# First phase of a two-block transformer kernel: both modulation vectors as column products on TensorE

## The chip, the cores and the metric

The kernel runs on one core of a Trainium2 chip, with float32 data. The metric is the device time of one execution in microseconds. A core has TensorE (PE, with its weight loads shown apart as PEld), VectorE (DVE), ScalarE (ACT), GpSimd (POOL) and SyncE (SP), each with its own instruction stream, tied together by semaphores; 16 DMA engines move data between HBM and the on-chip memory. TensorE writes to PSUM only.

## What is computed

Two blocks of layers on a sequence of 256 tokens of width 1024. What matters here is how the first one begins:

```python
def modulate(h, shift, scale):
    return h * (1.0 + scale[:, None, :]) + shift[:, None, :]

c_act = jax.nn.silu(c)
for i in range(DEPTH):
    mod = c_act @ ada_w[i] + ada_b[i]
    sh1, sc1, g1, sh2, sc2, g2, sh3, sc3, g3 = jnp.split(mod, N_MOD, axis=-1)
    h = modulate(rms_norm(x, ln_ffn1[i]), sh1, sc1)
    x = x + 0.5 * g1[:, None, :] * swiglu(h, ffn1_wg[i], ffn1_wu[i], ffn1_wd[i])
    ...
```

`sh1` is vector 0 of the kernel, `sc1` vector 1, `g1` vector 2. Each is a product of a row of 1024 with a 1024 x 1024 block of `ada_w`, 4 MB in float32. The first matrix product of the layer, `h @ wg`, needs vectors 0 and 1; `g1` is needed at the end of the layer.

## The kernel before

**Phases.** The program goes through ten phases, F0 (the first SwiGLU layer) first. Activations are kept with the feature on the partition: 8 blocks (`KB`) of 128 features by 256 tokens. Weights come in slabs of 128 x 2048, 1 MB each, into six slots (`raw`). ScalarE rounds a slab (`split_hi`), VectorE takes the remainder (`split_lo`), and TensorE makes three products for each pair of blocks: high by high, low by high, high by low.

**Vectors.** A block of `ada_w` comes as 8 tiles of 128 x 1024, 512 KB, each with two DMAs of 256 KB (`ada_load`, L2049). An interleaving is used: a tile holds `AG` = 2 halves j, each 128 partitions by 512 columns, where the parity of a partition tells which half of the output columns it holds. `ada_tile` (L2784, L2787) lets VectorE multiply a half by one column of c and add it to an accumulator, 16 steps for a vector. `ada_sum` (L2398) then sums over the partitions on TensorE: four calls with 128 columns of the accumulator stationary and the two columns of `group_ones` moving. The tiles are numbered m: vector 1 has 0 to 7, vector 0 has 8 to 15, vector 2 begins at 16. Tiles 4 to 11 lie in the slots of slabs 2 to 5, all others in the four slots of `ada` (m mod 4).

**The start, vector 1.** VectorE sums all 8 tiles into an accumulator of its own. `ada_sum(1)` puts it into PSUM (`first_summed`), and `mod_vector(1)` adds the bias (L2796).

**The start, vector 0.** VectorE sums tiles 8 to 11. For 12 to 15 (`PE_TILES` = 4) TensorE makes the product itself, `shift_tile` (L2499): two columns of `c_pair` stationary, 512 columns of the tile moving, into a 2 x 512 row in PSUM. `shift_start` (L2507) adds VectorE's part to the same row. ScalarE copies the row (L2626), `shift_turn` (L2514) transposes it in four pieces, and `mod_vector(0)` adds the bias. `c_pair` holds, for each of the 16 halves, a column of c masked by parity.

**TensorE's order at the start.** 16 transposes of x (L2524), 16 warm-up calls (`keep_warm`, L2406: ones by the identity into a bank that nobody reads), the sums of squares for rms_norm (L2425, 16 calls), 16 warm-up calls, six transposes of parameter rows (L2534), the spreading of 1/rms over the partitions (L2439), `ada_sum(1)`, 16 warm-up calls, the shift tiles and the turn, and then slab 0: `first_product` (L2297, L2303), which waits for the rounded operand (`norm_hi`). Slab 1 follows with `col_product` (L2270 to L2272).

**Queues.** SyncE issues c, x, the 16 tiles, and slabs 0 and 1; slab 0 goes ahead of tile 15. A load into a slot that is used again waits for `ada_step`, VectorE's count of steps. Slabs 2 to 5 wait for the tiles in their place. GpSimd issues the parameter rows, then vector 2's first four tiles (each waits for `ada_taken`, the count of tiles that TensorE has taken), then fills the table of distances for the attention phase (L2198, 32 copies, two DMAs), then vector 2's other tiles. VectorE sums vector 2 between the splits of F0.

Of the kernel before, what the change touches and what calls it, by code (L numbers as in the profile page):

```python
# [35 lines left out]
P = 128  # L36
# [3 lines left out]
KB = D // P  # L40
# [6 lines left out]
WARM = 8  # L47
ATILES = 4
AG = 2
AW = D // AG  # L50
AQ = P // AG
ASTEPS = KB * AG
PE_TILES = KB // 2
N_MOD = 9
# [53 lines left out]
def build(nc, T, out):  # L108
    phases = PHASES
    nslabs = sum(SLABS_OF.get(p, FFN_SLABS) for p in phases)  # L110
    with ExitStack() as ctx:
# [38 lines left out]
        def view(a, b):  # L150
            return work[:, a:b]
# [41 lines left out]
        def bank(t, j):  # L193
            return t[:, j * 512:(j + 1) * 512]
# [133 lines left out]
        out_rows = view(0, 2048)  # L328
        shift_row = view(5120, 5632)
        silu_sb = view(4096, 4608)  # L330
# [1671 lines left out]

        def acc_of(v):

            return view(8192, 8192 + AW) if v == 1 else ada_acc[:, 0:AW]

        first_summed, first_turned = bank(up, 1)[:, 0:KB], bank(up, 0)[:, 0:KB]

        def tile_index(v, k):

            return (v if v >= 2 else 1 - v) * KB + k

        def tile_steps(m):

            return AG * (m if m < 2 * KB else m - PE_TILES)

# [21 lines left out]
        def ada_load(eng, v, k, it=0, source=None):  # L2038
            m = tile_index(v, k)
            full = tile_full(m)[0]  # L2040
            if m >= 2 * KB + ATILES:
                eng.wait_ge(S["ada_step"], tile_steps(m - ATILES + 1) + ASTEPS * it)
            elif m >= 2 * KB:
                eng.wait_ge(S["ada_taken"], m - ATILES + 1 - (2 * KB - PE_TILES))
            elif m >= ATILES + 8:
                eng.wait_ge(S["ada_step"], tile_steps(m % ATILES + 1))
            source = ada_source(v, k) if source is None else source
            for j in range(AG):
                eng.dma_start(ada_place(m)[:, j * AW:(j + 1) * AW],  # L2049
                              source[j * AQ:(j + 1) * AQ, :].rearrange("q (g n) -> q g n", g=AG)).then_inc(full, 16)  # L2050

        @block.sync
        def _(sp):
            early_slabs = []
            def load(s, it, sources):

                if s >= RAW:
                    sp.wait_ge(lo_done, s - RAW + 1 + RAW * it)
                elif s >= 2:
                    sp.wait_ge(S["ada_step"], tile_steps(2 * s + 2))  # L2060
                for place, src in sources:
                    sp.dma_start(place(slab(raw, s, RAW)), src).then_inc(raw_full[s % RAW], 16)
# [47 lines left out]
            for k in range(KB):  # L2110
                if k == KB - 1:
                    load(0, 0, up_src(phases[0], 0, 0))
                ada_load(sp, 0, k)
# [58 lines left out]
        def _(pool):  # L2172
# [17 lines left out]
            link(pool.memset(rel_rows[0:HEADS, :], -1e30))  # L2190
            for k in range(ATILES):
                ada_load(pool, FIRST_VEC[phases[0]], k)
            pool.wait_ge(S["rel_rows"], 16)
# [24 lines left out]
            for p in phases:  # L2218
# [7 lines left out]
                if p in FFNS:  # L2226
                    if p in FIRST_VEC:
                        v = FIRST_VEC[p]
                        for k in range(ATILES, KB):
                            ada_load(pool, v, k)  # L2230
# [32 lines left out]
        def _(pe):  # L2263
# [127 lines left out]
            def ada_sum(v, it=0, o=bank(misc, 1)):  # L2391
# [5 lines left out]
                for h in range(KB // AG):  # L2397
                    last = pe.matmul(by_group[:, :, h], acc_of(v)[:, h * P:(h + 1) * P], group_ones[:, :],  # L2398
                                     start=True, stop=True, skip_group_check=True)
# [91 lines left out]

            def shift_tile(k):

                m = tile_index(0, k)
                full, count = tile_full(m)
                pe.wait_ge(full, count)
                for j in range(AG):
                    i = k * AG + j
                    last = pe.matmul(bank(misc, 1)[0:AG, :], c_pair[:, i * AG:(i + 1) * AG], ada_place(m)[:, j * AW:(j + 1) * AW],  # L2499
                                     start=(k == KB - PE_TILES and j == 0), stop=(k == KB - 1 and j == AG - 1),  # L2500
                                     skip_group_check=True)
                last.then_inc(S["ada_taken"], 1)

            def shift_start():

                pe.wait_ge(S["ada_step"], tile_steps(2 * KB - PE_TILES))
                pe.matmul(bank(misc, 1)[0:AG, :], group_ones[:, :], acc_of(0), start=False, stop=False, skip_group_check=True)  # L2507

            def shift_turn():

                pe.wait_ge(S["start_act"], 3)
                by_group = first_turned[:, 0:KB].rearrange("p (g h) -> p g h", g=AG)
                for h in range(KB // AG):
                    last = pe.transpose(by_group[:, :, h], shift_row[0:AG, h * P:(h + 1) * P], ident[0:AG, 0:AG])  # L2514
                last.then_inc(S["ada_summed"], 1)

# [5 lines left out]
            for k in range(KB):  # L2522
# [3 lines left out]
                if k % 2:  # L2526
                    last.then_inc(S["x_turned"], 1)
            keep_warm(bank(up, 0), 2 * WARM)
            norm_sums(phases[0], wide=False)
            keep_warm(bank(up, 0), 2 * WARM)  # L2530
            pe.wait_ge(S["rows_loaded"], 16 * len(rows_plan))
# [9 lines left out]
            pe.wait_ge(S["c_spread"], 2)  # L2541
            for k in range(KB - PE_TILES, KB):
                if k == KB - 1:
                    shift_start()
                shift_tile(k)
            shift_turn()
            for p in phases:
# [19 lines left out]
        def _(act):  # L2567
# [18 lines left out]
            def norm(name):  # L2586
# [30 lines left out]
                if n == 0:  # L2617
# [124 lines left out]
        def _(dve):  # L2742
# [28 lines left out]
            def ada_tile(v, k, it=0):  # L2771
# [4 lines left out]
                if k == 0 and v > 1:  # L2776
                    dve.wait_ge(S["ada_summed"], v + it)
                acc = acc_of(v)
                for j in range(AG):
# [18 lines left out]
            def norm(name):  # L2798
# [29 lines left out]
                if n == 0:  # L2828
                    split_lo(0)
                    mod_vector(0, psum=first_turned)  # L2830
                if name == "G":
# [90 lines left out]
            def ffn(p):  # L2922
# [92 lines left out]
                if v is not None and not more:  # L3015
# [10 lines left out]
                              group_ones[:, :].unsqueeze(1).to_broadcast([P, ASTEPS, AG]), ALU.mult).then_inc(S["c_spread"], 1)  # L3026
            for k in range(KB):
                ada_tile(1, k)
                if k == KB - 2:
                    dve.wait_ge(S["sqrt_done"], 1)  # L3030
                    dve.reciprocal(rstd, rstd).then_inc(S["rstd_done"], 1)
            for k in range(KB - PE_TILES):
                ada_tile(0, k)
            dve.wait_ge(S["start_act"], 2)
            for i, o in enumerate(OUT_COL.values()):
# [4 lines left out]
                                   float(NSA_HD) ** -0.5, ALU.mult, ALU.mult))  # L3040
            mod_vector(1, psum=first_summed)
            for p in phases:
# [26 lines left out]
```

## Time and profile before

| | us |
|---|---|
| median of 3 runs | 1780.62 |
| lowest, highest | 1780.35, 1782.24 |
| the profiled execution, its time | 1784.23 |
| the profiled execution, its span | 1782.6 |

Busy in the span: TensorE 1728.5 us, VectorE 1434.3, ScalarE 912.5, GpSimd 407.6. The DMA engines moved 411.44 MB, 231 GB/s in the mean. Times in the rows are counted from the span's start. A row of the timeline may merge several instructions (x32); its length is that of all of them. A float32 matmul of the program leaves two records of the weight load and two of the matmul. The granted clock is the share of 2.4 GHz that the throttle left to TensorE; 0.50 is 1.2 GHz.

### The profile page before, as it was taken

The page shows a single profiled execution, that of the slowest core. Times are in us where ns is not written, and L with a number is a line of the kernel's source. Part 1 is how long each engine was busy: PE and PEld are TensorE (multiplying, and loading weights), DVE is VectorE, ACT ScalarE, POOL GpSimd, SP SyncE. Part 2 cuts the span into 40 slices and gives each one's busy share as a digit, 9 for nine tenths or more (in the row PEclk, how much of TensorE's full clock was granted, in tenths as well). Part 3 has the DMA queues.
Part 4 walks back from the last instruction along what each step waited for, and adds up shares of the span by engine and source line. Part 5 has one row for each costly group of instructions (what it writes and reads, how often), then busy time and mean ns, then how long its engine had stood idle before and what let it go on. Part 6 is the DMA issues. An engine that isn't in the chain of part 4 may idle for free. (4 is left out here: it accounts for less than half of the span.)

```text
span 1782.6 us, 36482 instructions
## 1 busy us (share of the span) xinstructions
PE 1728.5 (97%) x14077; PEld 1682.8 (94%) x14077; DVE 1434.3 (80%) x1850; ACT 912.5 (51%) x1274; POOL 407.6 (23%) x669
## 2 busy tenths in 40 slices
PE   7999999999999999999999999899999998899998
PEld 6999999999999999989999998899999997699998
DVE  6777898688779888868977899869988998678555
ACT  3433377764335433456533366566444656665444
POOL 5322311013223222120122344411322121301000
PEclk9999999999999999999999999999999998999999
DMA  9998857448986888756698856335989592147550
GB/s 336 358 340 272 301 186 259 154 169 311 322 282 237 287 292 299 253 192 210 239 327 273 298 186 224 106 119 190 322 299 294 142 240 95 48 131 257 168 188 24
DMA packets 261792, 411.44 MB, mean 231 GB/s; under 512 B 21950, under 2 KB 204414, under 8 KB 261560
## 3 DMA queue, kind: packets, MB, share of 16 engines
q1 hardware_dynamic: 224968, 290.67, 49.1%
q0 software_dynamic: 36720, 119.36, 19.0%
q8 instruction: 69, 1.13, 0.3%
q14 instruction: 35, 0.29, 0.1%
HBM read 408.90 MB, written 2.63 MB: 231 GB/s over the span
## 5 line engine op out<-in xcount | busy, mean ns | idle before, releaser
L2751 DVE TENSOR_TENSOR lo<-raw,hi 128x2048 fp32r<-128x2048 f32 (+1 forms) x257 | 581.6, 2265 | 186.1 <-ACT hi L2578 185.8
L2578 ACT CAST hi<-raw 128x2048 fp32r<-128x2048 f32 (+1 forms) x266 | 498.7, 1878 | 393.2 <-PE dacc L2272 194.7
L2270 PE MATMUL up<-operand_hi,hi 128*128 128x256 f32 x1952 | 554.0, 284 | 4.0 <-DVE lo L2751 3.9
L2271 PE MATMUL up<-operand_lo,hi 128*128 128x256 f32 x1952 | 553.2, 283 | 0.0
L2272 PE MATMUL up<-operand_hi,lo 128*128 128x256 f32 x1952 | 553.0, 283 | 0.0
L2049 POOL DMA_DIRECT2D ada<-in_ada_w_dram x448 | 259.9, 597 | 816.9 <-DVE ada_acc L2787 753.4
L2270 PEld LDWEIGHTS up<-operand_hi,hi 128*128 128x128 f32 x1952 | 375.3, 192 | 5.5 <-DVE lo L2751 5.0
L2272 PEld LDWEIGHTS up<-operand_hi,lo 128*128 128x128 f32 x1952 | 375.4, 192 | 0.0
L2271 PEld LDWEIGHTS up<-operand_lo,hi 128*128 128x128 f32 x1952 | 375.3, 192 | 0.0
L2787 DVE SCALAR_TENSOR_TENSOR ada_acc<-ada,c_col,ada_acc 128x512 f32<-128x512 f32 x420 | 318.8, 759 | 13.5 <-DVE ada_acc L2787 0.5
L2270 PE MATMUL dacc<-act_hi,hi 128*128 128x256 f32 x1056 | 298.9, 283 | 2.6 <-DVE act_lo L2964 2.6
L2272 PE MATMUL dacc<-act_hi,lo 128*128 128x256 f32 x1056 | 298.5, 283 | 0.0
L2271 PE MATMUL dacc<-act_lo,hi 128*128 128x256 f32 x1056 | 297.8, 282 | 0.0
L2270 PEld LDWEIGHTS dacc<-act_hi,hi 128*128 128x128 f32 x1056 | 200.0, 189 | 3.2 <-issue 2.2
L2271 PEld LDWEIGHTS dacc<-act_lo,hi 128*128 128x128 f32 x1056 | 198.8, 188 | 0.0
L2272 PEld LDWEIGHTS dacc<-act_hi,lo 128*128 128x128 f32 x1056 | 198.0, 187 | 0.0
L2213 POOL TENSOR_TENSOR work<-work 128x256 f32<-128x256 f32 x52 | 40.1, 771 | 344.7 <-ACT work L2604 342.4
L2270 PE MATMUL dacc<-operand_hi,hi 128*128 128x256 f32 x352 | 101.3, 288 | 3.4 <-DVE operand_lo L843 2.4
L2272 PE MATMUL dacc<-operand_hi,lo 128*128 128x256 f32 x352 | 99.6, 283 | 0.0
L2271 PE MATMUL dacc<-operand_lo,hi 128*128 128x256 f32 x352 | 99.6, 283 | 0.0
L2680 ACT ACTIVATE work<-up 128x512 f32<-128x512 f32 x41 | 24.5, 598 | 136.0 <-PE up L2272 136.0
L2270 PEld LDWEIGHTS dacc<-operand_hi,hi 128*128 128x128 f32 x352 | 67.4, 192 | 4.7 <-issue 3.7
(455 smaller groups left out, 2716.0 us busy)
## 6 DMA issues: line engine op xcount, KB each, us to landing
ada<-in_ada_w_dram POOLq DMA_DIRECT2D x448, 256.0 KB, 4.6
raw<-in_ffn_wg_dram SPq DMA_DIRECT2D x88, 512.0 KB, 5.4
raw<-in_ffn_wu_dram SPq DMA_DIRECT2D x88, 512.0 KB, 5.0
raw<-in_ffn_wd_dram SPq DMA_DIRECT2D x88, 512.0 KB, 5.4
raw<-in_ffn_w_up_dram SPq DMA_DIRECT2D x88, 512.0 KB, 4.5
raw<-in_ffn_w_down_dram SPq DMA_DIRECT2D x46, 512.0 KB, 4.4
raw<-in_hg_w_in_dram SPq DMA_DIRECT2D x32, 512.0 KB, 5.9
raw<-in_attn_w_qkv_dram SPq DMA_DIRECT2D x24, 512.0 KB, 7.5
```

The lines of the kernel that those rows point to most:

```text
L2049: eng.dma_start(ada_place(m)[:, j * AW:(j + 1) * AW], source[j * AQ:(j + 1) * AQ, :].rearrange("q (g n) -> q g n", g=AG)).then_inc(full, 16)
L2213: ins = pool.tensor_tensor(acc, op_k(squares, 0) if k == 1 else acc, op_k(squares, k), ALU.add)
L2270: pe.matmul(o, stat[0], mov[0], start=start, stop=False, skip_group_check=True)
L2271: pe.matmul(o, stat[0], mov[1], start=False, stop=False, skip_group_check=True)
L2272: return pe.matmul(o, stat[1], mov[0], start=False, stop=stop, skip_group_check=True)
L2578: last = act.copy(put(slab(hi, s, SPL)), take(slab(raw, s, RAW)))
L2680: act.activation(silu_sb, bank(up, 0), ACT.Silu).then_inc(S["silu_done"], 1)
L2751: last = dve.tensor_tensor(put(slab(lo, s, SPL)), take(slab(raw, s, RAW)), put(slab(hi, s, SPL)).bitcast(F32), ALU.subtract)
L2787: dve.scalar_tensor_tensor(acc, t, c, acc, ALU.mult, ALU.add).then_inc(S["ada_step"], 1)
```

## The change

Vectors 1 and 0 both go through TensorE from the first tile to the last. `first_tile` takes a tile as it lies: 128 x 128 blocks of it are stationary, and the two columns of `c_pair` for this half move. A half has four such blocks, a tile eight, and all 64 calls of a vector add up in one 128 x 8 region of PSUM, which `mod_vector` reads. Behind each tile stand two warm-up calls. `first_done` is one more warm-up call whose end tells VectorE that the region is complete. VectorE's steps for vectors 1 and 0, the copy by ScalarE and the turn are gone. The loads that waited for `ada_step` wait for `ada_taken`. Slab 0 is issued ahead of tile 14 instead of tile 15. GpSimd loads vector 2 behind the table of distances and behind the first use of a slab (`slab_used`).

```diff
-PE_TILES = KB // 2
+PE_TILES = 2 * KB
...
-        first_summed, first_turned = bank(up, 1)[:, 0:KB], bank(up, 0)[:, 0:KB]
+        first_summed = {1: bank(up, 1)[:, 0:KB], 0: bank(misc, 1)[:, 0:KB]}
...
             elif m >= ATILES + 8:
-                eng.wait_ge(S["ada_step"], tile_steps(m % ATILES + 1))
+                eng.wait_ge(S["ada_taken"], m % ATILES + 1)
...
                 elif s >= 2:
-                    sp.wait_ge(S["ada_step"], tile_steps(2 * s + 2))
+                    sp.wait_ge(S["ada_taken"], 2 * s + 2)
...
-                if k == KB - 1:
+                if k == KB - 2:
                     load(0, 0, up_src(phases[0], 0, 0))
...
-            for k in range(ATILES):
-                ada_load(pool, FIRST_VEC[phases[0]], k)
             pool.wait_ge(S["rel_rows"], 16)
...
-                        for k in range(ATILES, KB):
+                        if p == phases[0]:
+                            pool.wait_ge(slab_used, 1)
+                        for k in range(0 if p == phases[0] else ATILES, KB):
                             ada_load(pool, v, k)
...
+            def first_tile(v, k):
+
+                m = tile_index(v, k)
+                full, count = tile_full(m)
                 pe.wait_ge(full, count)
+                by_group = first_summed[v].rearrange("p (g h) -> p g h", g=AG)
                 for j in range(AG):
                     i = k * AG + j
...
+                    for h in range(KB // AG):
+                        last = pe.matmul(by_group[:, :, h], ada_place(m)[:, j * AW + h * P:j * AW + (h + 1) * P],
+                                         c_pair[:, i * AG:(i + 1) * AG], start=(k == 0 and j == 0 and h == 0),
+                                         stop=(k == KB - 1 and j == AG - 1), skip_group_check=True)
                 last.then_inc(S["ada_taken"], 1)
...
+            def first_done():
+
+                pe.matmul(bank(up, 0)[:, 0:P], ones[:, :], ident[:, :], start=True, stop=True,
+                          skip_group_check=True).then_inc(S["ada_summed"], 1)
...
-            keep_warm(bank(up, 0), 2 * WARM)
+            pe.wait_ge(S["c_spread"], 2)
+            for k in range(5):
+                first_tile(1, k)
+                keep_warm(bank(up, 0), 2)
             norm_sums(phases[0], wide=False)
-            keep_warm(bank(up, 0), 2 * WARM)
+            for k in range(5, KB):
+                first_tile(1, k)
+                keep_warm(bank(up, 0), 2)
+            first_done()
...
-            ada_sum(1, o=first_summed)
-            keep_warm(bank(up, 0), 2 * WARM)
...
-            shift_turn()
+            for k in range(KB):
+                first_tile(0, k)
+                if k < KB - 1:
+                    keep_warm(bank(up, 0), 2)
+            first_done()
+            keep_warm(bank(up, 0), WARM // 2)
...
-                    act.wait_ge(S["ada_taken"], PE_TILES)
-                    act.copy(shift_row[0:AG, :], bank(misc, 1)[0:AG, :]).then_inc(S["start_act"], 1)
...
-            for k in range(KB):
-                ada_tile(1, k)
-                if k == KB - 2:
-                    dve.wait_ge(S["sqrt_done"], 1)
-                    dve.reciprocal(rstd, rstd).then_inc(S["rstd_done"], 1)
-            for k in range(KB - PE_TILES):
-                ada_tile(0, k)
+            dve.wait_ge(S["sqrt_done"], 1)
+            dve.reciprocal(rstd, rstd).then_inc(S["rstd_done"], 1)
```

TensorE, from the transposes of x to the first transpose of the parameter rows, before (x16 is that many calls; `ident,ones` is a warm-up call, `ones,work` a sum of squares):

```order
L2524 MATMUL dacc<-ident,work 128x128 x16
L2406 MATMUL up<-ident,ones 128x128 x16
L2425 MATMUL misc<-ones,work 128x128 x16
L2406 MATMUL up<-ident,ones 128x128 x16
L2534 MATMUL dacc<-ident,work 128x128
```

and of the changed kernel, from the same place to the sums of squares:

```order
L2513 MATMUL dacc<-ident,work 128x128 x16
L2496 MATMUL up<-c_pair,ada 128x2 x8
L2401 MATMUL up<-ident,ones 128x128 x2
L2496 MATMUL up<-c_pair,ada 128x2 x8
L2401 MATMUL up<-ident,ones 128x128 x2
L2496 MATMUL up<-c_pair,ada 128x2 x8
L2401 MATMUL up<-ident,ones 128x128 x2
L2496 MATMUL up<-c_pair,ada 128x2 x8
L2401 MATMUL up<-ident,ones 128x128 x2
L2496 MATMUL up<-c_pair,raw 128x2 x8
L2401 MATMUL up<-ident,ones 128x128 x2
L2420 MATMUL misc<-ones,work 128x128 x16
```

Five tiles now stand where one block of warm-up calls was; the other three of vector 1 follow the sums of squares.

TensorE, the end of the phase up to the first product of slab 0, before:

```order
L2398 MATMUL up<-group_ones,work 128x2 x4
L2406 MATMUL up<-ident,ones 128x128 x16
L2499 MATMUL misc<-ada,c_pair 2x512 x6
L2507 MATMUL misc<-ada_acc,group_ones 2x512
L2499 MATMUL misc<-ada,c_pair 2x512 x2
L2514 MATMUL up<-ident,work 128x2 x4
L2297 MATMUL up<-operand_hi,hi 128x256
```

and of the changed kernel, its last three tiles:

```order
L2496 MATMUL misc<-c_pair,ada 128x2 x8
L2401 MATMUL up<-ident,ones 128x128 x2
L2496 MATMUL misc<-c_pair,ada 128x2 x8
L2401 MATMUL up<-ident,ones 128x128 x2
L2496 MATMUL misc<-c_pair,ada 128x2 x8
L2503 MATMUL up<-ident,ones 128x128
L2401 MATMUL up<-ident,ones 128x128 x4
L2292 MATMUL up<-operand_hi,hi 128x256
```

The joining product and the four transposes are gone, and the closing call stands directly behind the last tile.

## Rows read from the trace of the kernel before

**Rows 1.** The page: busy us of an engine, share of the span, instructions.

```profile
PE 1728.5 (97%) x14077; PEld 1682.8 (94%) x14077; DVE 1434.3 (80%) x1850; ACT 912.5 (51%) x1274; POOL 407.6 (23%) x669
```

**Rows 2.** Waits of TensorE, 0 to 100 us: total, times, longest.

```profile
PE up L2270 <- DVE lo L2751: 2.0, 1, 2.0
```

**Rows 3.** Windows: PE, PEld, DVE, ACT, POOL busy; granted clock; DMA share; GB/s.

```profile
10.00:20.00 10.00, 10.00 (x92) 10.00 (x91) 9.04 (x13) 5.00 (x13) 4.92 (x10) 1.00 1.07 371
...
34.00:36.00 2.00, 1.16 (x4) 0.24 (x4) 0.39 (x1) 1.57 (x1) 0.83 (x2) 1.00 1.08 372
...
46.00:48.00 2.00, 1.11 (x7) 1.12 (x8) 0.83 (x1) 1.59 (x1) 1.70 (x6) 0.86 1.09 361
...
48.00:50.00 2.00, 2.00 (x11) 2.00 (x11) 1.66 (x1) 1.97 (x3) 1.88 (x3) 0.50 1.03 398
...
50.00:52.00 2.00, 2.00 (x16) 2.00 (x15) 0.63 (x1) 2.00 (x2) 1.53 (x5) 0.78 1.06 362
```

**Rows 4.** Timeline of the start: start us, us, engine, line, what [idle before].

```profile
9.74 0.49 DVE L2784 TENSOR_SCALAR work<-ada,c_col 128x512 f32<-128x512 f32 x1 [5.60 <-DMA ada<-in_ada_w_dram]
...
9.94 3.65 PEld L2406 LDWEIGHTS up<-ident,ones 128*128 128x128 f32 x32
...
20.77 0.98 PE L2534 MATMUL dacc<-ident,work 128*128 128x128 f32 x6
...
21.58 0.64 PE L2439 MATMUL misc<-ident,small 128*128 128x128 f32 x4
...
22.69 0.97 PEld L2398 LDWEIGHTS up<-group_ones,work 128*128 128x128 f32 x8 [0.66 <-DVE work L2787]
...
35.07 1.88 PE L2499 MATMUL misc<-ada,c_pair 128*2 128x512 f32 x4 [0.84 <-DMA ada<-in_ada_w_dram]
...
38.06 0.17 DVE L2796 TENSOR_TENSOR modcol<-up,cols 128x8 f32<-128x8 f32 x1 [0.16 <-PE up L2514]
...
38.91 0.35 PE L2297 MATMUL up<-operand_hi,hi 128*128 128x256 f32 x1 [0.89 <-ACT operand_hi L2634]
```

**Rows 5.** Timeline, product of slab 1.

```profile
46.88 0.39 PE L2270 MATMUL up<-operand_hi,hi 128*128 128x256 f32 x1 [1.99 <-DVE lo L2751]
...
48.11 0.41 PE L2271 MATMUL up<-operand_lo,hi 128*128 128x256 f32 x1
...
48.32 0.41 PE L2272 MATMUL up<-operand_hi,lo 128*128 128x256 f32 x1
...
51.84 0.28 PE L2271 MATMUL up<-operand_lo,hi 128*128 128x256 f32 x1
...
51.96 0.28 PE L2272 MATMUL up<-operand_hi,lo 128*128 128x256 f32 x1
```

**Rows 6.** Timeline of phase N: float32 rows with few moving columns.

```profile
1438.98 2.08 PE L1625 MATMUL dacc<-work 128*64 128x60 f32 x32
...
1453.04 3.65 PE L1638 MATMUL misc<-work 128*128 128x30 f32 x32
...
1456.63 3.26 PE L1625 MATMUL dacc<-work 128*64 128x60 f32 x32
```

**Rows 7.** Windows behind the second of those rows, columns as in 3.

```profile
1457.00:1458.00 1.00, 1.00 (x15) 1.00 (x13) 0.99 (x2) 0.52 (x1) 0.00 (x0) 0.58 0.12 45
...
1460.60:1461.00 0.40, 0.40 (x6) 0.40 (x5) 0.37 (x2) 0.00 (x0) 0.00 (x0) 1.00 0.89 174
```

**Rows 8.** Weight loads by form, 1505.0 to 1507.4 us, then 1495.0 to 1496.5.

```profile
L1694 PEld LDWEIGHTS dacc<-work 128*64 128x64 f32 x5 | 1.1, 231 | 0.5 <-issue 0.5
...
L1694 PEld LDWEIGHTS dacc<-work 128*64 128x64 f32 x8 | 1.0, 136 | 0.6 <-issue 0.3
```

**Rows 9.** Vector 2: a load, its first use; page, us to landing.

```profile
30.54 1.22 POOL L2049 DMA_DIRECT2D ada<-in_ada_w_dram  x2 [15.61 <-PE misc L2499]
...
64.83 0.48 DVE L2784 TENSOR_SCALAR ada_acc<-ada,c_col 128x512 f32<-128x512 f32 x1
...
ada<-in_ada_w_dram POOLq DMA_DIRECT2D x448, 256.0 KB, 4.6
```

More of the change, by code:

```diff
@@ L328, in build @@
         out_rows = view(0, 2048)
-        shift_row = view(5120, 5632)
         silu_sb = view(4096, 4608)
@@ L1999, in build @@
         PE_MIX["N"], ACT_MIX["N"], DVE_MIX["N"] = pe_nsa, act_nsa, dve_nsa
-        def acc_of(v):
-            return view(8192, 8192 + AW) if v == 1 else ada_acc[:, 0:AW]
-        first_summed, first_turned = bank(up, 1)[:, 0:KB], bank(up, 0)[:, 0:KB]
+        first_summed = {1: bank(up, 1)[:, 0:KB], 0: bank(misc, 1)[:, 0:KB]}
         def tile_index(v, k):
@@ L2013, in tile_steps @@
         def tile_steps(m):
-            return AG * (m if m < 2 * KB else m - PE_TILES)
+            return AG * (m - PE_TILES)
         def tile_full(m):
@@ L2043, in ada_load @@
             elif m >= 2 * KB:
-                eng.wait_ge(S["ada_taken"], m - ATILES + 1 - (2 * KB - PE_TILES))
+                eng.wait_ge(S["ada_taken"], m - ATILES + 1)
             elif m >= ATILES + 8:
-                eng.wait_ge(S["ada_step"], tile_steps(m % ATILES + 1))
+                eng.wait_ge(S["ada_taken"], m % ATILES + 1)
             source = ada_source(v, k) if source is None else source
@@ L2397, in ada_sum @@
                 for h in range(KB // AG):
-                    last = pe.matmul(by_group[:, :, h], acc_of(v)[:, h * P:(h + 1) * P], group_ones[:, :],
+                    last = pe.matmul(by_group[:, :, h], ada_acc[:, h * P:(h + 1) * P], group_ones[:, :],
                                      start=True, stop=True, skip_group_check=True)
@@ L2489, in ffn @@
                     ada_sum(v + 4)
-            def shift_tile(k):
-                m = tile_index(0, k)
+            def first_tile(v, k):
+                m = tile_index(v, k)
                 full, count = tile_full(m)
                 pe.wait_ge(full, count)
+                by_group = first_summed[v].rearrange("p (g h) -> p g h", g=AG)
                 for j in range(AG):
                     i = k * AG + j
-                    last = pe.matmul(bank(misc, 1)[0:AG, :], c_pair[:, i * AG:(i + 1) * AG], ada_place(m)[:, j * AW:(j + 1) * AW],
-                                     start=(k == KB - PE_TILES and j == 0), stop=(k == KB - 1 and j == AG - 1),
-                                     skip_group_check=True)
+                    for h in range(KB // AG):
+                        last = pe.matmul(by_group[:, :, h], ada_place(m)[:, j * AW + h * P:j * AW + (h + 1) * P],
+                                         c_pair[:, i * AG:(i + 1) * AG], start=(k == 0 and j == 0 and h == 0),
+                                         stop=(k == KB - 1 and j == AG - 1), skip_group_check=True)
                 last.then_inc(S["ada_taken"], 1)
[L2504 to L2515, printed above, removed]
+            def first_done():
+                pe.matmul(bank(up, 0)[:, 0:P], ones[:, :], ident[:, :], start=True, stop=True,
+                          skip_group_check=True).then_inc(S["ada_summed"], 1)
             pe.wait_ge(S["c_spread"], 1)
@@ L2538, in _ @@
             spread(misc[:, SEQ:2 * SEQ], rstd).then_inc(S["spread"], 1)
-            ada_sum(1, o=first_summed)
-            keep_warm(bank(up, 0), 2 * WARM)
[L2541 to L2545, printed above, removed]
-            shift_turn()
+            for k in range(KB):
[4 more added lines that the diff above has]
+            keep_warm(bank(up, 0), WARM // 2)
             for p in phases:
@@ L2777, in ada_tile @@
                     dve.wait_ge(S["ada_summed"], v + it)
-                acc = acc_of(v)
+                acc = ada_acc[:, 0:AW]
                 for j in range(AG):
@@ L2829, in norm @@
                     split_lo(0)
-                    mod_vector(0, psum=first_turned)
+                    mod_vector(0, psum=first_summed[0])
                 if name == "G":
@@ L3040, in _ @@
                                    float(NSA_HD) ** -0.5, ALU.mult, ALU.mult))
-            mod_vector(1, psum=first_summed)
+            mod_vector(1, psum=first_summed[1])
             for p in phases:
```

## The prediction

> **What bounds the kernel now.** I read the page first, then the waits of TensorE, then the first 50 us row by row. TensorE is busy for 97% of the span [rows 1], so what delays it is paid in full and what another engine saves is worth nothing unless TensorE waited for it. In the first 100 us it has few waits; the one that counts is 2.0 us for the remainder of slab 1 [rows 2]. Before the first product the start is paced by transfers. The DMA engines are full at 371 GB/s [rows 3], a tile of a modulation vector is 2 x 256 KB, so one lands every 0.524 MB / 371 GB/s = 1.41 us, and the last one lands just ahead of 35.07, where TensorE takes it up. VectorE keeps that pace, and the engine that has room is TensorE: most of its rows up to 28 us are warm-up products on constants (48 calls). After the last tile come 1.88 us of products, the copy of the row by ScalarE, four small transposes, the addition of the bias at 38.06 and the first product of slab 0 at 38.91 [rows 4]. I call that last moment T0. Everything the change does lies ahead of T0, apart from the wait for slab 1 and the clock just behind it. From there the program is the same, so the result is the move of T0, corrected for those two.
>
> **The unit of the sum.** A float32 matmul on a 128-column stationary leaves two records in the trace: 16 warm-up calls are 32 records. At the full clock (2.4 GHz) they follow each other every (3.65 - 0.19)/31 = 0.112 us. The new kind of product is already in the trace too, in the sum of vector 1: four calls with 128 stationary columns and two moving ones, 8 records, (0.97 - 0.19)/7 = 0.111 us apart [rows 4]. So a product that moves two columns costs as much as one that moves 128; its weight load sets the time. I use 0.112 for both. The old shift products (2 stationary columns, 512 moving) cost 1.88 us for 4 records, one tile: 16 records of the new kind in a tile cost 1.79 us, about the same.
>
> **What is removed.** From TensorE: 48 warm-up calls, the sum of vector 1 (8 records), four tiles of the old form with their join, and four small transposes, all ahead of T0. Of these only what follows the last landing was on the path. From VectorE: 12 tile sums of vectors 1 and 0. They ran beside the transfers at the pace of the landings and did not set T0, so nothing is gained there. The way from the last old product (35.07 + 1.88 = 36.95) to the bias at 38.06 loses its copy and its turn, 1.1 us, if the last tile were still what ends the phase. It isn't, as the next sum shows.
>
> **What is added.** Per tile 8 calls, 16 records; 16 tiles are 256 records. Two warm-up calls behind each tile but the last: 15 x 4 = 60. The sums of squares stay, 32, and two closing calls add 4. That is 352 records. The six transposes of parameter rows and the two that spread rstd keep about 1.3 us [rows 4]. A tile with its warm-up calls takes 20 x 0.112 = 2.24 us where one lands every 1.41. TensorE becomes the bound of the whole phase, and the tiles of both vectors stand in one line on it.
>
> **T0 at the full clock.** TensorE is free of the x transposes at about 10.05 and tile 0 has landed by 9.74 [rows 4]. 10.05 + 352 x 0.112 (39.4) + 1.3 = 50.8. From the bias to the first product it took 0.85 us before; with the hop from the closing call I take 0.9. T0 = 51.7, which is 12.8 later than 38.91. The four warm-up calls ahead of slab 0 (0.9) fit into that hop.
>
> **The clock.** The new rows load weights nearly all the time and move few columns. Very similar rows exist in the later part of this kernel: 32 records with 128 stationary and 30 moving columns from 1453.04, back to back, then 32 with 64 and 60 [rows 6]. TensorE never idled there, and yet the granted clock went from 1.00 to 0.50 (1.2 GHz) about 4.1 us after they began, and back at about 1460.6, once dense products ran again [rows 7]. Twenty of those records move 600 columns; twenty of the new ones, warm-up calls included, move 16 x 2 + 4 x 128 = 544. So I expect the low level here as well. How long a record takes there: dense products with 128 columns loaded stood 0.21 us apart at 0.50 (48.11 to 48.32) against 0.12 at 1.00 (51.84 to 51.96, [rows 5]), and a load of 64 columns took 231 ns instead of 136 at a place where the moving side was the longer one [rows 8], so the loads themselves slow down. No row shows a two-column product at the low clock. From below it costs 0.112 as at full clock, from above 0.213, double the nearest row; I take 0.213, since the load is what sets it and the load was seen to slow by about that step.
>
> The page "TensorE: Matmul & The Clock Gate" of the Trainium skill, section "LDWEIGHTS (loading the stationary operand)", gives a load as columns / 1.2 ns with no mention of the clock's state, thus 107 ns; the trace agrees at full clock (0.111) and speaks against it at the low one (231 ns against 136). That rule is the second rival below.
>
> **T0 with the clock as those rows had it.** I let it fall 4 us after a run of tiles begins and return 4 us after dense rows begin. First five tiles from 10.05: 36 records until 14.1, then 64 x 0.213 = 13.6, to 27.7. Sums of squares: 19 records low, 13 at full, 5.5, to 33.2. Three tiles: 36 records, then 24 low, to 42.3. Closing call, transposes and spread, all taken double: 3.0, to 45.3. Eight tiles: 156 x 0.213 = 33.2, to 78.5. Closing call 0.4 and hop 0.9: T0 = 79.8, which is 40.9 later. Dense rows began at 78.5, so slab 0 runs at the low clock until 82.5, 2.7 us, and loses 2.7 x (1 - 0.12/0.213) = 1.2.
>
> **Behind T0.** Before, TensorE waited 1.99 us ahead of 46.88 for slab 1 [rows 5], and its clock was at 0.50 for 3.4 us soon after (0.86, 0.50 and 0.78 in [rows 3]), which cost 3.4 x (1 - 0.12/0.213) = 1.5. In the new kernel slabs 0 and 1 have landed long ahead. With slab 0 slowed no wait is left, so 2.0 + 1.5 = 3.5 is given back; at the full clock ScalarE still rounds slab 1 after the eight operand rows, and I leave 1.0 of the 2.0 (bounds 0 and 2). Net: 40.9 + 1.2 - 3.5 = **+38.6 us**.
>
> **Moved at no cost.** GpSimd no longer waits for tiles before its table of distances, and loads vector 2 once slab 0 has been used, about 6 us after T0. A tile is two issues, 1.22 us together (four tiles: 4.9), and lands 4.6 us after its issue in the median [rows 9], so four tiles are there by T0 + 16. VectorE first uses one at 64.83, T0 + 26 [rows 9]: ten microseconds of cover; without it VectorE would hold back the next split by what is missing. Queued behind GpSimd's wait are only these loads. SyncE's loads of slabs 2 to 5 now wait for tiles taken by TensorE instead of VectorE; tile 12 is taken before T0 by several tiles, so they land under the phase.
>
> **The rivals.** *Full clock throughout:* the warm-up calls hold it. For it speaks that between 34 and 36 us TensorE was busy for 1.16 of 2 us and the clock stayed at 1.00 [rows 3], and that the new phase has no gap. Against it, rows 6 and 7. It gives 12.8 - 1.0 - 1.5 = +10.3. The same page, in "Why this matters for your kernels", ties drops to idle gaps between bursts; by that rule this rival would be the outcome, but the clock fell at 1457 with TensorE busy throughout. *The clock falls, the loads don't slow:* only records that move 128 columns double. That adds to 51.7: 49 warm-up records in the low stretches (244 x 4/20) x 0.1 = 4.9, sums of squares 1.9, transposes and closing calls 1.7; T0 = 60.2, net 21.3 + 1.2 - 3.5 = +19.0. This also stands for a clock that is low for part of the time only. *Faster:* the load of the next two-column product hides, and TensorE keeps pace with the landings. It decides at (1.41 - 0.45)/16 = 0.060 us for a record; that is the step of records with 64 stationary columns ((2.08 - 0.22)/31, [rows 6]), not of 128. T0 would be 10.05 + 256 x 0.060 + 96 x 0.112 + 1.3 + 0.9 = 38.4, -0.5, and net -0.5 - 1.0 - 1.5 = -3.0; with faster records still the last landing limits it to about -4.
>
> **How the numbers follow.** The profiled execution has a span of 1782.6 and a time of 1784.23, 3.6 over the median of the runs, 1780.62. The shifts are in microseconds of the same work, so I add them to the median. Low clock: 66%, 1780.6 + 38.6 = 1819.2. Partly low, or loads not slowed: 12%, 1799.6. Full clock: 18%, 1790.9. TensorE keeps pace: 4%, 1777. About 0.2% (3.6 us) is what a measurement of this kernel can tell from no change; the last case lies on that border and is split: faster 0.02, same 0.02, slower 0.96. If all of the phase ran at the low clock: 352 x 0.213 + 2.6 + 10.05 + 0.9 = 88.6, net +47.4, 1828. The range takes in this and the full-clock rival with 2 us below it: 1789 to 1828.
>
> **What would show it.** The granted clock in the windows from 14 to 78 us: 0.50 in most for the forecast, 1.00 for the first rival. The new product line: 0.213 us a record at the low clock, 0.112 at full; a record of 0.112 at 0.50 is the second rival. The first product of slab 0 at about 80 (forecast), 60, 52 or 38. No wait for slab 1, no wait of VectorE for vector 2. The forecast fails if the clock holds, or if the records are shorter than the four in the sum of vector 1.

## The result, and the profile after

| | before | changed |
|---|---|---|
| median, us | 1780.63 (4 runs) | 1822.56 (4 runs) |
| lowest, highest | 1780.35, 1782.24 | 1821.91, 1824.48 |
| span of the profiled execution | 1782.6 | 1820.3 |

The ratio is 1.023, 95% interval 1.0216 to 1.0243: 41.9 us slower between the medians, 37.7 between the two profiled spans. The forecast was 1819.2 (+38.6).

TensorE in the first 100 us of the changed kernel has no wait behind the arrival of x; the wait for slab 1 of [rows 2] is gone. The granted clock tells the rest (windows of the changed kernel; columns as in [rows 3]):

```profile
12.00:16.00 4.00, 4.00 (x27) 4.00 (x28) 0.00 (x0) 3.39 (x10) 3.63 (x12) 0.71 1.06 367
16.00:20.00 4.00, 4.00 (x21) 4.00 (x21) 0.00 (x0) 0.00 (x0) 2.96 (x18) 0.50 1.06 367
...
28.00:32.00 4.00, 4.00 (x20) 4.00 (x20) 0.00 (x0) 0.00 (x0) 0.57 (x1) 0.50 1.08 365
32.00:36.00 4.00, 4.00 (x29) 4.00 (x29) 0.17 (x1) 0.26 (x1) 0.00 (x0) 0.73 1.05 426
36.00:40.00 4.00, 4.00 (x38) 4.00 (x37) 0.00 (x0) 0.00 (x0) 0.00 (x0) 1.00 0.98 307
40.00:44.00 4.00, 4.00 (x24) 3.60 (x23) 0.00 (x0) 0.00 (x0) 0.00 (x0) 0.62 0.98 315
44.00:48.00 4.00, 4.00 (x21) 4.00 (x20) 2.28 (x10) 3.07 (x8) 0.00 (x0) 0.50 0.63 219
...
72.00:76.00 4.00, 4.00 (x20) 4.00 (x21) 0.00 (x0) 0.00 (x0) 0.00 (x0) 0.50 0.00 0
...
80.00:84.00 4.00, 4.00 (x29) 4.00 (x28) 3.23 (x8) 4.00 (x8) 0.00 (x0) 0.76 0.00 0
```

TensorE is busy for 4.00 of 4.00 us in every one of these windows and yet has 20 or 21 products in a window at 0.50 where it has 38 in the one at 1.00. The clock is at 0.50 from 13.7 to 34.2 and from 41.0 to 82.0 us.

The timeline of TensorE, the rows that answer to [rows 4] (L2496 is the column product, L2401 a warm-up call):

```profile
7.44 3.32 PE L2513 MATMUL dacc<-ident,work 128*128 128x128 f32 x16 [3.63 <-DMA work<-in_x_dram]
10.60 1.84 PE L2496 MATMUL up<-c_pair,ada 128*128 128x2 f32 x16
...
29.12 6.14 PE L2420 MATMUL misc<-ones,work 128*128 128x128 f32 x32
35.10 1.84 PE L2496 MATMUL up<-c_pair,raw 128*128 128x2 f32 x16
37.33 1.84 PE L2496 MATMUL up<-c_pair,raw 128*128 128x2 f32 x16
...
45.26 3.41 PE L2496 MATMUL misc<-c_pair,raw 128*128 128x2 f32 x16
...
49.52 3.41 PE L2496 MATMUL misc<-c_pair,raw 128*128 128x2 f32 x16
52.80 1.20 PE L2401 MATMUL up<-ident,ones 128*128 128x128 f32 x4
53.79 3.41 PE L2496 MATMUL misc<-c_pair,raw 128*128 128x2 f32 x16
...
75.12 3.41 PE L2496 MATMUL misc<-c_pair,ada 128*128 128x2 f32 x16
78.40 0.77 PE L2503 MATMUL up<-ident,ones 128*128 128x128 f32 x2
78.97 1.91 PE L2401 MATMUL up<-ident,ones 128*128 128x128 f32 x8
80.53 0.56 PE L2292 MATMUL up<-operand_hi,hi 128*128 128x256 f32 x1
```

A tile with its two warm-up calls takes 37.33 - 35.10 = 2.23 us at the full clock and 53.79 - 49.52 = 4.27 at the low one: 20 records of 0.112 and of 0.213. The sixteen tiles follow each other without a gap on TensorE, with the sums of squares and the transposes of the parameter rows between them, and slab 0 begins at 80.53 instead of 38.91. Behind it, the same instruction of VectorE, the remainder of the first hidden activations, first in the kernel before, then in the changed one:

```profile
55.81 0.69 DVE L2964 TENSOR_TENSOR act_lo<-work,act_hi 128x512 fp32r<-128x512 f32 x1 [0.69 <-ACT act_hi L2695]
```

```profile
94.32 0.69 DVE L2955 TENSOR_TENSOR act_lo<-work,act_hi 128x512 fp32r<-128x512 f32 x1 [0.69 <-ACT act_hi L2686]
```

94.32 - 55.81 = 38.51 us: of the 41.6 by which slab 0 starts later, 3.1 are given back within the first two slabs, and from here to 750 us the two traces run side by side at that distance, within 0.04. Behind that it shrinks to 37.7 in three small steps, near 757, 801 and 1623 us of the trace of before. The windows around them have the clock at 1.00 in both traces, so the clock is not their reason, and what it is stays open.

### The profile page after: what moved, and what is told of

Read it like the earlier page. It is cut to its first block and busy times, and to the rows that moved or that the text cites. A ratio compares the mean times of both kernels' runs of the same rounds, so it can differ in the third digit from the quotient of the medians.

```text
span 1820.3 us, 36852 instructions
## 1 busy us (share of the span) xinstructions
PE 1771.7 (97%) x14279; PEld 1733.1 (95%) x14279; DVE 1416.9 (78%) x1826; ACT 911.5 (50%) x1273; POOL 400.9 (22%) x669
## 5 line engine op out<-in xcount | busy, mean ns | idle before, releaser
L2778 DVE SCALAR_TENSOR_TENSOR ada_acc<-ada,c_col,ada_acc 128x512 f32<-128x512 f32 x420 | 318.9, 759 | 13.7 <-DVE ada_acc L2778 0.6
```

The source lines that it names most:

```text
L2778: dve.scalar_tensor_tensor(acc, t, c, acc, ALU.mult, ALU.add).then_inc(S["ada_step"], 1)
```

## The experiments

Three kernels ask for the clock, the other runs for the rest of the change and for what stays open. "Before" is run with each batch; its medians were 1782.1, 1782.6 and 1780.7 us in the three, with single executions from 1778.0 to 1786.6, so comparisons go by the ratio within a batch.

**Move 128 columns instead of two.** The columns of c are repeated 64 times. The load and the 16 records of a tile's products stay, the warm-up calls behind the tiles go. The result is wider, so the addition of the bias picks its two columns out of each 128.

```diff
-                        last = pe.matmul(by_group[:, :, h], ada_place(m)[:, j * AW + h * P:j * AW + (h + 1) * P],
-                                         c_pair[:, i * AG:(i + 1) * AG], start=(k == 0 and j == 0 and h == 0),
+                        last = pe.matmul(first_summed[v][:, h * P:(h + 1) * P].rearrange("p (r g) -> p r g", g=AG),
+                                         ada_place(m)[:, j * AW + h * P:j * AW + (h + 1) * P],
+                                         c_pair[:, i * AG:(i + 1) * AG].unsqueeze(1).to_broadcast([P, WIDE, AG]), start=(k == 0 and j == 0 and h == 0),
```

> The changed kernel with 128 columns moving instead of 2: the two columns of c_pair are repeated 64 times, into four 128-column regions of the bank, of which two columns each are read. The warm-up calls behind the tiles are taken out. The output is the reference's. Clock theory (a record costs 0.112 us at the full clock whether it moves 2 or 128 columns, and the rows with few moving columns let the clock fall): the granted clock stays at 1.00, 292 records x 0.112 = 32.7 from 10.6, + 1.3 + 0.9, slab 0's first product at about 45.5, time 1785 (1783 to 1788). Rival (the phase is long for another reason: waits for tiles, the weight load itself slower from tiles than from the accumulator): first product at 65 to 80, time 1805 to 1822.

Measured: 1788.23 us (6 runs), ratio to before 1.0031 (1.0014 to 1.0048), about +5.5 us. The windows and the timeline:

```profile
20.00:24.00 4.00, 4.00 (x39) 4.00 (x38) 0.00 (x0) 0.25 (x1) 2.42 (x11) 1.00 1.05 383
...
36.00:40.00 4.00, 4.00 (x38) 4.00 (x37) 1.56 (x1) 0.00 (x0) 0.00 (x0) 1.00 0.97 294
```

```profile
30.42 7.31 PE L2496 MATMUL misc<-c_pair,raw 128*128 128x128 f32 x64
37.57 7.31 PE L2496 MATMUL misc<-c_pair,ada 128*128 128x128 f32 x64
...
45.99 0.35 PE L2293 MATMUL up<-operand_hi,hi 128*128 128x256 f32 x1
```

Four tiles are 64 records in 7.15 us, 0.112 each, with 64 times as many columns moved. Slab 0 begins at 45.99 against 45.5 expected, and from 12 us on the clock is at 1.00 by the windows and by the records both; the first two microseconds of tiles ran slower, with 11 products from 10 to 12 us. The clock theory holds: of the 42 us, some 36 go with the clock and the 60 warm-up records (6.7 at full clock) that this kernel leaves out; what is left is TensorE's 1.79 us for a tile that lands every 1.41. The next kernel leaves out the same records and moves two columns. The two differ only in the columns moved and in how the bias picks up the result, so the step between them, 1788.23 against 1811.28, is that of the columns.

**Leave the warm-up calls out.**

```diff
             for k in range(5):
                 first_tile(1, k)
-                keep_warm(bank(up, 0), 2)
             norm_sums(phases[0], wide=False)
             for k in range(5, KB):
                 first_tile(1, k)
-                keep_warm(bank(up, 0), 2)
             first_done()
...
                 first_tile(0, k)
-                if k < KB - 1:
-                    keep_warm(bank(up, 0), 2)
             first_done()
```

> The changed kernel without the two warm-up calls behind each tile, nothing else. Clock theory: they did not hold the clock, so the 60 records go at 0.213 us each: first product 12.8 earlier than 80.5, at 67.7, time 1822.6 - 12.8 = 1810. Rival (they keep part of the phase at the full clock): the time stays within 3 us of 1822.6 or rises.

Measured: 1811.28 us (1805.8 to 1818.5, 4 runs), ratio 1.0159 (1.0129 to 1.019), so 11 us under the changed kernel by the medians and 13 by the ratios, with 12.8 expected. By the times the warm-up calls cost their records and held nothing. The trace is less clear. In it slab 0 began at 73.31, not 67.7, and TensorE had the full clock for 3.4 us of the phase, where it had it for 10 in the changed kernel. Whether the missing calls or this one execution made that difference is not shown.

The clock did not come up at the x transposes at all, and the first 23 us of tiles ran at the low level. This is read from the records, not from the clock column:

```profile
10.26 13.65 PE L2496 MATMUL up<-c_pair,ada 128*128 128x2 f32 x64
```

```profile
12.00:16.00 4.00, 4.00 (x20) 4.00 (x20) 0.00 (x0) 3.10 (x10) 3.63 (x12) 1.00 1.06 365
...
34.00:38.00 4.00, 4.00 (x32) 4.00 (x31) 0.17 (x1) 0.12 (x1) 0.00 (x0) 0.81 0.96 364
44.00:48.00 4.00, 4.00 (x22) 4.00 (x20) 3.52 (x13) 2.40 (x5) 0.00 (x0) 0.50 0.63 211
```

From 12 to 16 us the column says 1.00, but there are 20 products, as many as at 0.50 elsewhere, and the first 64 records take 13.65 us, 0.213 each. In this trace the column stands at 1.00 from the start until the first fall that it shows, at 36.5 us, though the records go from 0.213 to 0.112 at 33.1. So ahead of the first change in a trace the column alone proves nothing, and the distance of the records has to be looked at with it.

**Eight warm-up calls instead of two.** 180 more records.

```diff
-                keep_warm(bank(up, 0), 2)
+                keep_warm(bank(up, 0), 8)
```

(in all three places)

> The changed kernel with eight warm-up calls instead of two behind each tile: 180 more records. Clock theory: the denser mix keeps the clock at 1.00, 532 records x 0.112 = 59.6 from 10.6, + 1.3 + 0.9, first product at 72.4, time 1822.6 - 8 = 1814, faster although work is added. Rival (cost goes by the number of records, the clock is not what matters or still falls): 180 x 0.213 = 38 later, time 1861.

Measured: 1813.3 us (1811.7, 1811.8, 1814.8 and 1830.2), ratio 1.0205 (1.0165 to 1.0244). Slab 0 begins at 72.09, expected 72.4, and all windows of the phase are at 1.00:

```profile
28.00:32.00 4.00, 4.00 (x39) 4.00 (x38) 0.00 (x0) 0.03 (x1) 0.50 (x1) 1.00 1.08 364
...
60.00:64.00 4.00, 4.00 (x37) 4.00 (x37) 0.00 (x0) 0.00 (x0) 0.00 (x0) 1.00 1.09 357
```

```profile
65.45 1.84 PE L2496 MATMUL misc<-c_pair,ada 128*128 128x2 f32 x16
67.16 2.03 PE L2401 MATMUL up<-ident,ones 128*128 128x128 f32 x16
...
72.09 0.35 PE L2292 MATMUL up<-operand_hi,hi 128*128 128x256 f32 x1
```

Each tile has 32 records instead of 20 and takes 3.58 us instead of 4.27. In the phase more work takes less time, 8.4 us less, and the rival's 38 us more are far off. This tells the clock from the count of records more sharply than anything else here. For the whole kernel the gain is not shown: three of the four executions lie 8 to 11 us under the median of the changed kernel, but one lies above it, and the interval of the ratio takes in the changed kernel's 1.023.

**The part on GpSimd's queue alone.** The kernel before, with vector 2's loads behind the table of distances and behind slab 0:

```diff
-            for k in range(ATILES):
-                ada_load(pool, FIRST_VEC[phases[0]], k)
             pool.wait_ge(S["rel_rows"], 16)
...
-                        for k in range(ATILES, KB):
+                        if p == phases[0]:
+                            pool.wait_ge(slab_used, 1)
+                        for k in range(0 if p == phases[0] else ATILES, KB):
                             ada_load(pool, v, k)
```

> The kernel before with one part of the change alone: GpSimd loads vector 2 behind the table of distances and behind the first use of a slab. Transfer theory (the 2.1 MB of vector 2 lay ahead of slab 1 and delayed it by up to 2.1 MB / 371 GB/s = 5.6 us): the wait of 2.0 us for slab 1 goes, the clock no longer falls behind it (1.5 us), time 1777 (1776 to 1779). Rival (slab 1 came late for another reason, or the clock falls anyway): no change, 1780.6 within 0.7.

> The same kernel as e1_pool, on the chip of this batch, to compare e5 and e6 with. The wait of 2.0 us for slab 1 is gone and the clock falls once, ahead of or under slab 0: -1 to -2 us against the kernel before, ratio 0.9990 to 0.9995. If it comes out at 1.0000 or above, the wait that went is paid back elsewhere.

Measured: 1780.8 us and 0.9992 (0.9981 to 1.0004) the first time, 1780.41 and 0.9988 (0.9979 to 0.9996) the second, 12 runs each: -1.4 and -2.1 us. The first interval takes in no change, the second just does not; the 1777 us expected were not reached. The wait for slab 1 fell from 2.0 to nothing and to 0.8. Windows of the first, where TensorE's longest wait behind 10 us is 0.9, for ScalarE's first operand row:

```profile
38.00:40.00 2.00, 1.26 (x10) 1.29 (x11) 1.43 (x5) 1.91 (x5) 0.00 (x0) 1.00 1.10 348
40.00:42.00 2.00, 2.00 (x12) 2.00 (x11) 1.91 (x5) 2.00 (x5) 0.00 (x0) 0.50 1.13 413
42.00:44.00 2.00, 2.00 (x13) 2.00 (x13) 0.79 (x1) 2.00 (x2) 0.00 (x0) 0.65 0.99 407
```

The wait is gone and the clock fell all the same, now under slab 0. In the second execution of the same program it did not fall there. The 1.5 us that I had charged to the wait for slab 1 thus do not hang on that wait alone. The two executions also show where single executions of this kernel come to differ by some microseconds. Their spans are 1782.1 and 1776.3, and the windows of the later phases differ in the clock, first of the one, then of the other:

```profile
336.00:340.00 4.00, 3.79 (x20) 3.82 (x21) 2.07 (x6) 3.15 (x9) 0.00 (x0) 0.62 0.37 130
1183.00:1187.00 4.00, 4.00 (x23) 4.00 (x23) 1.56 (x3) 0.00 (x0) 0.00 (x0) 0.57 0.70 241
```

```profile
336.00:340.00 4.00, 4.00 (x35) 4.00 (x36) 2.32 (x5) 3.13 (x9) 0.00 (x0) 1.00 0.27 92
1183.00:1187.00 4.00, 4.00 (x37) 4.00 (x35) 0.64 (x1) 1.36 (x2) 0.00 (x0) 1.00 0.00 0
```

**Fill the gaps ahead of slab 0.** e1_pool with warm-up calls where TensorE waits for ScalarE:

```diff
+            keep_warm(bank(up, 0), 3)
             shift_turn()
+            keep_warm(bank(dacc, 0), 4)
```

> e1_pool with three warm-up calls while ScalarE copies the shift row and four behind the turn, where TensorE sits idle anyway; nothing else. If the gaps between the shift products and slab 0 are what lets the clock fall under slab 0 (39.98 to 43.40 us in e1_pool), it stays at 1.00 and the time is 1.5 us under e1_pool, ratio to before 0.998. If the shift products themselves (two stationary columns, 28 to 37 us) are what lowers it, the clock falls as in e1_pool and the time is that of e1_pool.

Measured: 1782.51 us, ratio 0.9992 (0.9982 to 1.0002). The clock stayed at 1.00 from 38 to 44 us, but it did so in the second execution of e1_pool too, without the calls. Slab 0 began at 39.28 against 38.74. Inconclusive on the clock, and no gain.

**Column products only for the last four tiles.** The kernel before with the moved loads, and tiles 12 to 15 as column products with 128 columns moving. VectorE's sum of tiles 8 to 11 joins as four more products; copy and turn are gone, and three warm-up calls stand ahead of slab 0.

```diff
                 for j in range(AG):
                     i = k * AG + j
-                    last = pe.matmul(bank(misc, 1)[0:AG, :], c_pair[:, i * AG:(i + 1) * AG], ada_place(m)[:, j * AW:(j + 1) * AW],
+                    for h in range(KB // AG):
+                        last = pe.matmul(wide_out(h), ada_place(m)[:, j * AW + h * P:j * AW + (h + 1) * P],
+                                         wide_in(c_pair[:, i * AG:(i + 1) * AG]),
...
-                    act.wait_ge(S["ada_taken"], PE_TILES)
-                    act.copy(shift_row[0:AG, :], bank(misc, 1)[0:AG, :]).then_inc(S["start_act"], 1)
```

> The kernel before with vector 2's loads moved as in e1_pool, and the last four tiles of vector 0 as column products with 128 columns moving; VectorE's share of vector 0 joins them as four more products, the bias is added straight from PSUM as soon as the last tile is taken. Theory (where the last landing ends the phase, the copy and the turn are worth 1.1 us, and columns moving without a pause hold the clock): first product at 37.9 against 38.9, no wait for slab 1 (2.0), clock at 1.00 behind it (1.5), together -4.5 us against the kernel before of the same batch, ratio 0.9975. Rival (the column tiles at 1.79 us do not keep up with the last landings, or the clock falls at the wait for the last tile all the same): first product at 38.5 to 39.5, -1 to -2.5 us, ratio 0.9985 to 0.9995.

Measured: 1780.69 us, ratio 0.9988 (0.9978 to 0.9998), no better than the moved loads alone, where I had expected 0.9975. The timeline tells why the copy and the turn were worth nothing:

```profile
33.79 1.90 ACT L2589 CAST hi<-raw 128x2048 fp32r<-128x2048 f32 x1 [4.41 <-DMA raw<-in_ffn_wg_dram]
35.20 2.05 PE L2509 MATMUL misc<-c_pair,ada 128*128 128x128 f32 x16 [0.58 <-DMA ada<-in_ada_w_dram]
35.72 2.29 DVE L2760 TENSOR_TENSOR lo<-raw,hi 128x2048 fp32r<-128x2048 f32 x1 [2.71 <-ACT hi L2589]
37.09 0.39 PE L2524 MATMUL up<-ident,ones 128*128 128x128 f32 x2
37.93 0.16 DVE L2802 TENSOR_TENSOR modcol<-misc,cols 128x8 f32<-128x8 f32 x1
38.78 0.36 PE L2306 MATMUL up<-operand_hi,hi 128*128 128x256 f32 x1 [0.63 <-ACT operand_hi L2643]
```

The last tile is done at 37.1, but the bias (L2802) comes at 37.93, where VectorE has come through the split of slab 0 (L2760), 2.29 us from 35.72; in VectorE's program the split stands ahead of the bias. So it stood before:

```profile
35.61 2.29 DVE L2751 TENSOR_TENSOR lo<-raw,hi 128x2048 fp32r<-128x2048 f32 x1 [2.73 <-ACT hi L2578]
```

There the split ran to 37.9, and the bias came at 38.06, 0.16 us later, behind the turn [rows 4]. All but these 0.16 us of the copy and the turn were hidden beside it.

**The same with two columns moving.**

```diff
-        WIDE = 64
+        WIDE = 1
```

> e5_hybrid with 2 columns moving instead of 128 in the last four tiles, nothing else; the number of records is the same. Clock theory: from about 28 to 37 us few columns move, the clock falls in or just behind that stretch and rows run at 0.213 instead of 0.112 for some 3.4 us or more, so the time is 1.5 to 6 us over e5_hybrid. Rival (a run of four tiles is too short to matter): equal to e5_hybrid within 0.7 us.

Measured: 1783.96 us (10 runs), ratio 1.0008 (0.9997 to 1.0019), 3.3 over e5_hybrid. In the trace the clock fell at 30.6, two microseconds into the four tiles, and stayed down until 47.7; slab 0 began at 44.00. This is the slowest of the ten executions (1789.86 us; the others 1782.0 to 1785.6), so it shows the effect larger than it is in the median.

```profile
28.00:32.00 4.00, 3.33 (x24) 3.36 (x25) 3.83 (x13) 0.31 (x1) 2.64 (x7) 0.82 1.09 361
32.00:36.00 4.00, 4.00 (x20) 4.00 (x20) 1.47 (x4) 1.72 (x1) 0.00 (x0) 0.50 1.08 362
```

```profile
28.67 8.64 PE L2509 MATMUL misc<-c_pair,ada 128*128 128x2 f32 x48 [1.28 <-DMA ada<-in_ada_w_dram]
44.00 0.56 PE L2306 MATMUL up<-operand_hi,hi 128*128 128x256 f32 x1
```

Forty-eight records take 8.64 us, in e5_hybrid 5.60, where the clock stays at 1.00 through the phase. The two kernels differ in nothing but the number of columns moved, and four tiles are enough to set it off.

**Slab 0 one tile earlier**, on top of e5_hybrid, the line of the change on SyncE's queue:

```diff
-                if k == KB - 1:
+                if k == KB - 2:
                     load(0, 0, up_src(phases[0], 0, 0))
```

> e5_hybrid with slab 0 issued ahead of tile 14 instead of tile 15 (the one line of the change on that queue). In e5_hybrid the last tile was taken at 37.09 but the bias came at 37.93, directly behind VectorE's split of slab 0. Theory (that split bounds the phase there): it ends some 1.4 us earlier, the bias comes at 37.2, the first product at 38.1 instead of 38.78, time 0.7 us under e5_hybrid. Rival (the last tile lands later by what slab 0 gains): the first product stays at 38.6 to 39.2 and the time is that of e5_hybrid.

Measured: 1784.17 us, ratio 1.0012 (1.0002 to 1.0021), about 4 us slower than e5_hybrid by the ratios. The rival was right, and by more than it said:

```profile
34.37 2.05 PE L2509 MATMUL misc<-c_pair,ada 128*128 128x128 f32 x16 [1.82 <-DMA ada<-in_ada_w_dram]
37.15 1.95 PE L2509 MATMUL misc<-c_pair,ada 128*128 128x128 f32 x16
39.14 0.17 DVE L2802 TENSOR_TENSOR modcol<-misc,cols 128x8 f32<-128x8 f32 x1 [1.92 <-PE misc L2509]
```

The split now ends at 37.2, but tile 14 is taken at 34.37, behind a wait of 1.8 us, and tile 15 at 37.15 instead of 35.20. The bias comes at 39.14, 1.2 us later than in e5_hybrid. From 86 to 339 us the two traces run 1.22 us apart; then the distance becomes 2.7, where the clock of this execution is at 0.76 from 336 to 340 us and that of e5_hybrid at 1.00. The part of the 4 us beyond the 1.2 is thus not shown to come from the edit. The DMA engines were full here (a share of 1.04 and above from 22 to 38 us), and the tiles behind the slab landed later by more than the slab gained: tile 14 by an estimated 2.6 us (34.37 against about 31.8, two thirds into the 48 records of e5_hybrid), while the split of slab 0 came 0.8 us earlier. In the changed kernel the same line costs nothing: its last tile was issued by 27.5 us and TensorE takes it at 75.12.

**The changed kernel once more.**

> The changed kernel once more, beside e9_early_slab on one chip. Theory: the low clock from about 14 us to slab 0 repeats, first product at 80 to 82, 38 to 42 us over the kernel before. If the low stretch depended on the moment at which the program starts, it would come out under 1815 in some executions.

Measured: 1819.93 us (1815.8 to 1827.2, 4 runs), ratio 1.0219 (1.0192 to 1.0247). The low clock repeats, from 13.0 to 33.5 and from 40.3 to 81.3 us.

## Why the prediction was right

Point by point, by its own steps:

- **The unit.** 0.112 us for a record at the full clock, whether it moves 2 or 128 columns: 20 records in 2.23 us, and 64 wide ones in 7.15. Right.
- **TensorE becomes the bound of the phase.** Right. The sixteen tiles run from 10.60 to 78.4 us without a gap, and TensorE waited for none of them.
- **The record at the low clock.** No row of before showed it; 0.213 was taken from between 0.112 and 0.213. Measured: 4.27 us for 20. So the double of the nearest row was the right choice, and the second rival, loads that don't slow down, falls with it. The page "TensorE: Matmul & The Clock Gate" of the Trainium skill (section "LDWEIGHTS (loading the stationary operand)") gives a load of 128 columns 107 ns and doesn't speak of the clock's state; that fits the 0.112 at full clock and not the 0.213 at the low one.
- **The clock's course.** Set at "falls 4 us after a run of tiles begins, returns 4 us after dense rows begin". It fell 3.1 us after the first tile (10.60 to 13.7), returned 5.0 us after the sums of squares began (29.12 to 34.2) and fell 5.9 us after the second run began (35.10 to 41.0). Each is off by 1 to 2 us, with both signs, and by the middle of the phase they had cancelled, together with x landing 0.7 later (7.44 against 6.7): the tiles of vector 0 began at 45.26, forecast 45.3, and ended at 78.40, forecast 78.5.
- **The end of the phase.** T0 came out at 80.53 against 79.8, and the 0.7 lie behind the last tile. I gave the closing call and the hop 1.3 us and let the four warm-up calls fit into it, by their 0.9 at full clock. At the low clock their 8 records ran from 78.97 to 80.5, and slab 0 began directly behind them: 2.13 us. The prediction put these calls at nothing where they were the last thing on the path.
- **The first rival.** Full clock throughout had slab 0 at 51.7 and fails; e4_warm8 shows that the clock can be held by such calls, but by eight for a tile and not by two.
- **What is given back.** Forecast 3.5 less 1.2 for slab 0 at the low clock, 2.3 net; measured 3.1. The clock returned at 82.0, 1.5 us into slab 0 instead of 2.7, which makes that term 0.6; the rest of the 0.8 is 0.2 more given back than the 3.5. The sum of the steps, 38.6, stands against 38.51 at the instruction where the two traces become parallel. That the agreement is so close is luck: T0 was 0.7 too small and the part given back 0.8, and the errors of the clock's course cancelled ahead of both.
- **A mis-sized piece without effect.** I called the copy and the turn worth 1.1 us if the last tile ended the phase. e5_hybrid and the row at 35.61 show that VectorE's split of slab 0 ended only 0.16 us ahead of the bias, so that was their worth. It did not enter the sum, since the tiles end the phase here.
- **Moved at no cost.** Right for vector 2: four tiles were issued from 87.46 on, and VectorE took up the first at 103.33 without a wait. Moved alone, those loads gave 1.4 and 2.1 us, the only part of the change that was seen to give anything.
- **Median against span.** The median moved by 41.9, the span by 37.7. The profiled execution of before was 3.6 over its median, and the same program scatters by up to 8 us between executions. The repeated run gave a ratio of 1.0219, some 39 us. So the times bear out the forecast to within a few microseconds, not to within tenths.

The best versions are the kernel before with vector 2's loads moved (0.9988, 0.9979 to 0.9996, in the second comparison) and e5_hybrid (0.9988, 0.9978 to 0.9998). Both intervals reach close to 1, and they do not differ from each other.

What stays open: whether the gaps between the last tile and slab 0 lower the clock in the kernel before. It fell there in one execution of e1_pool and not in the other, and no kernel here separated the two.

## What to carry to other kernels

A product with a full stationary block of 128 columns and two moving ones cost as much here as one that moves 128 (0.112 us a record at full clock), and a run of them let TensorE's clock fall although the engine never idled; look in the trace for such rows and read the granted clock behind them before moving work of this form onto TensorE. If the form is needed, let it move more columns, since these were free here. Read the clock column together with the distance of the records. Compare the cost of a piece with the interval at which its data lands: 1.79 us against 1.41 made this change slower even at the full clock (e2_wide, +5.5 us).

## What was not expected of the hardware

- Useless work bought time in the phase: 180 extra records made it 8.4 us shorter (80.53 to 72.09), since the clock stayed at 1.00 with them.
- In one execution (e3_nowarm) TensorE ran at the low clock from its first products to 33 us, though it was busy all the time from 6.8 us on, and the clock column read 1.00 there.
- Two executions of the same program differed by 5.8 us in span (1782.1 and 1776.3), with the clock at 0.50 in places where the other had 1.00, as at 336 and 1183 us.
